# Fox attention normalised after the value product: blocks of ones beside the values give the row sums

## The chip, the core and the metric

The kernel runs on one core of a Trainium2 chip: TensorE (PE) for matrix products and transposes, VectorE (DVE) and ScalarE (ACT) for elementwise work, GpSimd (POOL), and queues that issue transfers (SP's and ACT's matter here). The engines run side by side and meet at semaphores. The metric is the device time of one execution in microseconds (us), of which the median of several runs is taken.

## The reference, cut to what matters

The kernel computes one step of a one-layer decoder: a projection into four branches, their merge, cross attention and a feed-forward part, for a prompt of 512 tokens and 8 sample tokens. The change touches branch D, the forgetting attention of the prompt: 8 heads of 64 over 512 tokens, causal.

```
def forgetting_attention(q, k, v, c_q, c_k, q_pos, k_pos):
    ...
        s = jnp.einsum('bqhd,bkhd->bhqk', qi, k, preferred_element_type=F32) * (d ** -0.5)
        s = s + jnp.swapaxes(ci, 1, 2)[..., None] - ck
        s = jnp.where(k_pos[None, None, None, :] <= pi[None, None, :, None], s, NEG_INF)
        p = jax.nn.softmax(s, axis=-1)
        return jnp.einsum('bhqk,bkhd->bqhd', p.astype(v.dtype), v)
```

## The kernel before

The weights of all projections are cut into pieces of 128 columns. For every piece `p` TensorE makes two halves (`("piece", p, 0)` and `("piece", p, 1)`), each of 24 products of 128x260 (12 for a piece of `w_branch` or `w_co`, whose weights have 512 rows): three products a block of rows, since weights and activations are split in a high and a low part (`wh`, `rawl`, `xh`, `xl`).

Everything else is a list of side steps, `SIDE`. The function `timeline()` puts one side step behind each half piece, and every engine walks the same list. The side step K works so: ACT and DVE do their part of step K on what TensorE left in PSUM in step K-1, and TensorE's part of step K waits for both (`act_s`, `dve_s`). While ACT and DVE work, TensorE does the half piece that stands between step K-1 and step K. So their part costs nothing as long as it is shorter than the half piece.

The steps of the stage are, in this order: `kvt` 0 to 4 transposes values and keys of the prompt, one block of 128 tokens a step, ACT copies the values into `vt` and the keys into `stg` and issues a store of each from its queue. `fc` makes the running sums of the forget gate. `fox` 0 to 34 is the attention, a pipeline over 32 (head, block of 128 queries) pairs. The logits of pair n are made in step n (PSUM bank `s0`, width w of 128, 256, 384 or 512 keys by the block, so the widths repeat with a period of four steps), the row maximum, the exponential into `fP` and the scaling in step n+1, the transpose of `fP` into bank `s1` also in step n+1, its copy to `fPT` and the product with `vt` into bank `s2` in step n+2, and the copy of `s2` to the branch's result `oD` in step n+3. Between them the paged values of the sample tokens pass (`("v", n)`, and `("vx", b)` each four of them). Their pages come by SP's queue, and DVE works on them at L1970 and L1974.

A step of DVE in `fox` is: row maximum (L1707), copy of the last but one pair's result (L1711), then wait for ACT's exponential, reciprocal of its 128x1 row sums (L1714), and the scaling of `fP` (the helper's line L1519). ACT has the exponential with the row sums as an accumulated second output (L1145) and then the copy to `fPT` (L1323).

The pieces end before the attention does. The steps `fox` 28 to 34 and then `df` (DVE, sample tokens) stand in the list without a half piece between them, because the pieces of branch D's own weights must come after. Then `split brD` follows: ACT copies `oD` to `oh`, DVE subtracts to get `ol`.

Of the kernel before, what the change touches and what calls it, by code (L numbers as in the profile page):

```python
# [18 lines left out]
ACT = mybir.ActivationFunctionType  # L19
# [382 lines left out]
def to_dve(s):  # L402

    kind, n = s[0], s[1]
    if kind == "fox":
        return int(1 <= n <= FOX)
    if kind == "x":
        return int(1 <= n <= XU)
    if kind == "l2" or kind == "gp":
        return int(n > 0)  # L410
    return {("sm", 2): 1, ("sm", 3): 1, ("fc", 1): 1, ("gdn", 0): 2, ("cln", 5): 1, ("cln", 6): 4, ("ds", 2): 1, ("dn", 1): 1,
            ("xd", 2): 1}.get((kind, n), 0)
# [19 lines left out]
def build(nc, a, out):  # L432
    ctx = ExitStack()
    with ctx:
# [144 lines left out]
        zrow = v(G + 1024, T)  # L579
        vt = v(G, QT, 512)  # L580
        fP, fPT = v(G + 2048, 512), v(G + 2560, QT, P)
        stg = v(G + 4096, 2, 512)
# [217 lines left out]
        def _(pe):  # L800
            def mm(o, l, r, start=True, stop=True):
                return pe.matmul(o, l, r, start=start, stop=stop, skip_group_check=True)  # L802
# [109 lines left out]
            def side(K, s):  # L912
# [56 lines left out]
                elif kind == "fox":  # L969
# [11 lines left out]
                    if 2 <= n <= FOX + 1:  # L981
                        h, q = divmod(n - 2, QT)
                        for b in range(q + 1):
                            last = mm(s2[FD * (h % 2):FD * (h % 2) + FD, 0:P], vt[:, b, h * FD:(h + 1) * FD], fPT[:, b, :], b == 0, b == q)
                elif kind == "l2":
# [152 lines left out]
        def _(act):  # L1138
# [5 lines left out]
            def fn(o, i, f, st=act_c, **kw):  # L1144
                own(act.activation(o, i, f, **kw), st)  # L1145
# [107 lines left out]
            def side(K, s):  # L1253
# [40 lines left out]
                elif kind == "kvt":  # L1294
                    j = (n - 1) % 2
                    rows = lambda x: x[0, (n - 1) * P:n * P].rearrange("t l h d -> t (l h d)")
                    fn(vt[:, n - 1, :], s0, ACT.Copy)
                    store(rows(out["fv_p"]), vt[:, n - 1, :], vt_out)
                    if used[j]:
# [16 lines left out]
                elif kind == "fox":  # L1316
                    if n <= FOX:
                        w = ((n - 1) % QT + 1) * P
                        act.wait_ge(v2a.sem, va + 1)
                        fn(fP[:, 0:w], s0[:, 0:w], ACT.Exp, a2v, bias=nmx[:, 0:1], accum_out=rsum[:, 0:1])  # L1320
                    w = ((n - 2) % QT + 1) if 2 <= n <= FOX + 1 else 1
                    if 2 <= n <= FOX + 1:
                        fins = act.activation(fPT[:, 0:w, :], s1[:, 0:w * P].rearrange("p (a b) -> p a b", a=w), ACT.Copy)  # L1323
                    else:
                        fins = act.activation(rsum[:, 1:2], eps6[:, 0:1], ACT.Copy)
                elif kind == "l2":
                    if n == 0:
# [75 lines left out]
                elif kind == "ml" and n == 0:  # L1403
                    act.wait_ge(gs_out, 16)
                    act.wait_ge(ss_st, 32)
                    act.wait_ge(vt_out, 64)
                    for j in range(2):
# [97 lines left out]
            act.wait_ge(ss_st, 32)  # L1505
            act.wait_ge(vt_out, 64)


        @block.vector
        def _(dve):  # L1510
# [146 lines left out]
            def side(K, s):  # L1657
# [46 lines left out]
                elif kind == "fox":  # L1704
# [3 lines left out]
                    if n >= 3:  # L1708
                        h, q = divmod(n - 3, QT)
                        r = slice(FD * (h % 2), FD * (h % 2) + FD)  # L1710
                        (dve_c if n <= FOX else dve_s).by(dve.tensor_copy(oD[r, h // 2, q * P:(q + 1) * P], s2[r, 0:P]))  # L1711
                    if n <= FOX:
                        dve.wait_ge(a2v.sem, av + 1)
                        own(dve.reciprocal(nmx[:, 1:2], rsum[:, 0:1]))  # L1714
                        ts(fP[:, 0:w], fP[:, 0:w], nmx[:, 1:2], st=dve_s)
                elif kind == "l2":
# [293 lines left out]
```

## Time and profile before

| | |
|---|---|
| median of 3 runs | 1835.05 us (1833.76 to 1837.18) |
| the profiled execution: its time, its span | 1833.14 us, 1831.3 us |
| busy over the span: PE, DVE, ACT, POOL | 84%, 51%, 30%, 27% |
| mean granted TensorE clock | 0.893 of full |
| the steps `kvt`, `fc` and `fox` lie at | about 836 to 1086 us of the span |

The busy share of PE is that of pipelined products, so it counts overlapping ones once and does not say that the engine is at its peak. The granted clock takes two values, full and half, and its mean says how much of the span was at each.

### The profile page before, as it was taken

Reading aid. Unit: us, or ns where it says so; the run is one execution under the profiler, and the core shown is the slowest. Engines: PE = TensorE matmul, PEld = TensorE weight load, DVE = VectorE, ACT = ScalarE, POOL = GpSimd, SP = SyncE. Lnnn points to the kernel's source line nnn. Section 1 sums busy time; section 2 is a strip of 40 time slices with the busy share of each in tenths; the row PEclk is TensorE's granted clock in tenths of the full one; section 3 lists DMA queues with packets and bytes.
Section 4 is the critical chain, followed back from the end, with each engine's and each line's share of the span. In section 5 each row is a group of like instructions: output and inputs, shape, how many; then the busy total and the mean of one; then the engine's idle time right before and its main releaser. Section 6 shows DMA issues by size and latency. Waiting matters only on the chain. (4 is left out here: it accounts for less than half of the span.)

```text
span 1831.3 us, 28404 instructions
## 1 busy us (share of the span) xinstructions
PE 1546.3 (84%) x11127; PEld 1424.3 (78%) x11127; DVE 942.1 (51%) x1421; ACT 555.5 (30%) x893; POOL 489.8 (27%) x286
## 2 busy tenths in 40 slices
PE   4896577878797978988899879889577999999996
PEld 4896577678796977877666659888476999999995
DVE  4169877999977754223222222264525566663122
ACT  3322441122224212263222232443214333333222
POOL 1253312234343400001111104310402444443440
PEclk8897786899898989999888879989757999999998
DMA  7145423433453416557343006432312233332331
GB/s 213 47 118 154 127 76 103 125 107 115 116 150 104 133 54 203 147 159 223 115 126 99 24 21 194 127 89 87 127 35 75 81 93 93 93 93 77 98 97 47
DMA packets 250997, 199.86 MB, mean 109 GB/s; under 512 B 11620, under 2 KB 208797, under 8 KB 250456
## 3 DMA queue, kind: packets, MB, share of 16 engines
q1 hardware_dynamic: 234149, 169.47, 31.9%
q10 hardware_dynamic: 15723, 23.86, 3.8%
q0 software_dynamic: 992, 4.72, 0.8%
q8 instruction: 88, 1.44, 0.3%
q14 instruction: 45, 0.37, 0.1%
HBM read 187.89 MB, written 10.81 MB: 108 GB/s over the span
## 5 line engine op out<-in xcount | busy, mean ns | idle before, releaser
L802 PE MATMUL pb<-xh,wh 128*128 128x260 f32 x2176 | 647.8, 298 | 48.7 <-DVE xl L1516 22.6
L802 PE MATMUL pb<-xl,wh 128*128 128x260 f32 x2176 | 631.9, 290 | 0.0
L802 PE MATMUL pb<-xh,rawl 128*128 128x260 f32 x2176 | 630.6, 290 | 0.0
L762 POOL TENSOR_TENSOR rawl<-raw,wh 128x1024 fp32r<-128x1024 f32 (+2 forms) x128 | 277.8, 2171 | 930.5 <-ACT wh L1145 930.3
L802 PEld LDWEIGHTS pb<-xh,wh 128*128 128x128 f32 x2176 | 428.5, 197 | 66.0 <-issue 34.9
L802 PEld LDWEIGHTS pb<-xl,wh 128*128 128x128 f32 x2176 | 428.4, 197 | 0.7
L802 PEld LDWEIGHTS pb<-xh,rawl 128*128 128x128 f32 x2176 | 427.7, 197 | 0.0
L1145 ACT ACTIVATE wh<-raw 128x1024 fp32r<-128x1024 f32 (+2 forms) x208 | 201.6, 969 | 557.0 <-PE pb L802 531.0
L802 PE MATMUL sd<-ar 128*128 128x128 f32 (+5 forms) x1584 | 282.7, 374 | 93.0 <-DVE ar L1516 33.8
L802 PEld LDWEIGHTS sd<-ar 128*128 128x128 f32 (+4 forms) x1584 | 199.9, 199 | 139.6 <-issue 78.1
L773 POOL TENSOR_TENSOR ar<-ar 128x512 f32<-128x512 f32 x128 | 182.2, 1423 | 333.1 <-DMA ar<-in_cache_fox_k 317.3
L1631 DVE TENSOR_TENSOR rawl<-raw,wh 128x1024 fp32r<-128x1024 f32 (+1 forms) x80 | 94.7, 1184 | 70.8 <-ACT wh L1145 70.6
L802 PE MATMUL pb<-oh,wh 128*128 128x260 f32 (+1 forms) x384 | 123.2, 321 | 7.3 <-ACT ar L1145 4.7
L802 PE MATMUL pb<-ol,wh 128*128 128x260 f32 (+1 forms) x384 | 116.7, 304 | 0.0
L802 PE MATMUL pb<-oh,rawl 128*128 128x260 f32 (+1 forms) x384 | 116.4, 303 | 0.0
L806 PE MATMUL sd<-cst,ar 128*128 128x128 f32 (+7 forms) x359 | 68.0, 316 | 51.6 <-DVE ar L1516 24.9
L802 PE MATMUL pb<-hh,wh 128*128 128x260 f32 x352 | 100.9, 287 | 2.6 <-DVE hl L1516 2.6
L1648 DVE SCALAR_TENSOR_TENSOR ar<-xT,cols,ar 128x512 f32<-128x512 f32 x120 | 102.0, 882 | 1.4 <-DVE ar L1516 0.3
L802 PE MATMUL pb<-hh,rawl 128*128 128x260 f32 x352 | 100.2, 285 | 0.0
L802 PE MATMUL pb<-hl,wh 128*128 128x260 f32 x352 | 100.1, 284 | 0.0
L1145 ACT ACTIVATE ar<-ar 128x520 f32<-128x520 f32 (+8 forms) x71 | 41.7, 587 | 190.2 <-DVE ar L1542 166.1
L1655 DVE TENSOR_REDUCE ar<-ar 128x8 f32<-128x512 f32 x128 | 85.2, 678 | 26.5 <-POOL ar L773 25.8
(168 smaller groups left out, 1756.9 us busy)
## 6 DMA issues: line engine op xcount, KB each, us to landing
raw<-in_w_in SPq DMA_DIRECT2D x80, 512.0 KB, 4.1
ar<-in_cache_fox_k SPq DMA_DIRECT2D x128, 256.0 KB, 2.7
ar<-in_cache_fox_v SPq DMA_DIRECT2D x128, 256.0 KB, 3.1
raw<-in_w_ffn_in SPq DMA_DIRECT2D x44, 512.0 KB, 3.7
raw<-in_w_branch SPq DMA_DIRECT2D x32, 256.0 KB, 3.2
raw<-in_w_ffn_out SPq DMA_DIRECT2D x16, 512.0 KB, 3.9
ar<-in_cache_mem_k ACTq DMA_DIRECT2D x1, 4096.0 KB, 19.2
raw<-in_w_out SPq DMA_DIRECT2D x8, 512.0 KB, 4.0
```

The source lines that it names most:

```text
L762: pool.tensor_tensor(rawl[:, p % RING, 0:kt, :], raw[:, p % RING, 0:kt, :], wh[:, p % (AHEAD + 1), 0:kt, :].bitcast(F32), SUB).then_inc(lo ...
L773: own(pool.tensor_tensor(kring[:, i % 4, :], kring[:, i % 4, :], qb[:, :], MUL), prod_done)
L802: return pe.matmul(o, l, r, start=start, stop=stop, skip_group_check=True)
L806: return pe.transpose(o, i, ident[0:n, 0:n])
L1145: own(act.activation(o, i, f, **kw), st)
L1631: dve.tensor_tensor(rawl[:, p % RING, 0:kt, :], raw[:, p % RING, 0:kt, :], wh[:, p % (AHEAD + 1), 0:kt, :].bitcast(F32), SUB).then_inc(lo. ...
L1648: dve_c.by(dve.scalar_tensor_tensor(out=oC[:, c, 0:SEQ], in0=g[:, j - 1:j - 1 + SEQ], scalar=w[:, j - 1:j], in1=oC[:, c, 0:SEQ], op0=MUL, ...
L1655: page_free.by(dve.tensor_reduce(sc[:, i, :], kring[:, i % 4, :].rearrange("p (h d) -> p h d", h=FH), AX, ADD))
```

## The change

The row sums no longer come from ACT's accumulator, and the exponentials are no longer scaled. The tile `vt` gets blocks of ones between the values of an even and an odd head (192 columns for two heads: 64 of values, 64 ones, 64 of values). The product for a head takes 128 of these columns where it took 64, so that its result has 64 partitions of sums of values and 64 of row sums. DVE takes the reciprocal of the 64x128 row sums, read from PSUM, into a new tile `frs`, and multiplies with it as it moves the result to `oD`. ACT does its copy to `fPT` first and the exponential after it. The values leave for DRAM in two stores of 256-byte rows for each block of tokens, instead of one of 2 KB rows.

```diff
--- before.py
+++ after.py
@@ -402,8 +402,6 @@
 def to_dve(s):
 
     kind, n = s[0], s[1]
-    if kind == "fox":
-        return int(1 <= n <= FOX)
     if kind == "x":
         return int(1 <= n <= XU)
     if kind == "l2" or kind == "gp":
@@ -577,8 +575,8 @@
         wsh = nc.alloc_sbuf_tensor_at("wsh", [P, KD, 16], F32R, offset=base + 4 * (G + 128))
         wsl = nc.alloc_sbuf_tensor_at("wsl", [P, KD, 16], F32R, offset=base + 4 * (G + 256))
         zrow = v(G + 1024, T)
-        vt = v(G, QT, 512)
-        fP, fPT = v(G + 2048, 512), v(G + 2560, QT, P)
+        vt = v(G, QT, 4 * 192)
+        fP, fPT, frs = v(G + 3072, 512), v(G + 3584, QT, P), v(SQ, P)
         stg = v(G + 4096, 2, 512)
 
         cnh = nc.alloc_sbuf_tensor_at("cnh", [P, 512], F32R, offset=base + 4 * (G + 5632))
@@ -981,7 +979,7 @@
                     if 2 <= n <= FOX + 1:
                         h, q = divmod(n - 2, QT)
                         for b in range(q + 1):
-                            last = mm(s2[FD * (h % 2):FD * (h % 2) + FD, 0:P], vt[:, b, h * FD:(h + 1) * FD], fPT[:, b, :], b == 0, b == q)
+                            last = mm(s2[:, 0:P], vt[:, b, 192 * (h // 2) + FD * (h % 2):192 * (h // 2) + FD * (h % 2) + 2 * FD], fPT[:, b, :], b == 0, b == q)
                 elif kind == "l2":
                     for j in range(2):
                         for h in range(2):
@@ -1294,8 +1292,11 @@
                 elif kind == "kvt":
                     j = (n - 1) % 2
                     rows = lambda x: x[0, (n - 1) * P:n * P].rearrange("t l h d -> t (l h d)")
-                    fn(vt[:, n - 1, :], s0, ACT.Copy)
-                    store(rows(out["fv_p"]), vt[:, n - 1, :], vt_out)
+                    vb = vt[:, n - 1, :].rearrange("p (c e d) -> p c e d", c=4, e=3)
+                    fn(vb[:, :, 1, :], spread(ones[:, 0:FD], 4, 1), ACT.Copy)
+                    for e in range(2):
+                        fn(vb[:, :, 2 * e, :], s0.rearrange("p (c e d) -> p c e d", c=4, e=2)[:, :, e, :], ACT.Copy)
+                        store(rows(out["fv_p"]).rearrange("t (c e d) -> t c e d", c=4, e=2)[:, :, e, :], vb[:, :, 2 * e, :], vt_out)
                     if used[j]:
                         act.wait_ge(stg_out[j], 16 * used[j])
                     fn(stg[:, j, :], s1, ACT.Copy)
@@ -1314,15 +1315,19 @@
                     fn(pn[:, :, :], pn[:, :, :], ACT.Exp, a2v)
                     fins = act.activation(rsum[:, 0:1], eps6[:, 0:1], ACT.Copy)
                 elif kind == "fox":
-                    if n <= FOX:
-                        w = ((n - 1) % QT + 1) * P
-                        act.wait_ge(v2a.sem, va + 1)
-                        fn(fP[:, 0:w], s0[:, 0:w], ACT.Exp, a2v, bias=nmx[:, 0:1], accum_out=rsum[:, 0:1])
+                    if n == 1:
+                        act.wait_ge(ss_st, 32)
                     w = ((n - 2) % QT + 1) if 2 <= n <= FOX + 1 else 1
                     if 2 <= n <= FOX + 1:
                         fins = act.activation(fPT[:, 0:w, :], s1[:, 0:w * P].rearrange("p (a b) -> p a b", a=w), ACT.Copy)
                     else:
                         fins = act.activation(rsum[:, 1:2], eps6[:, 0:1], ACT.Copy)
+                    if n <= FOX:
+                        act_c.by(fins)
+                        w = ((n - 1) % QT + 1) * P
+                        act.wait_ge(v2a.sem, va + 1)
+                        act.wait_ge(act_c.sem, act_c.n)
+                        fins = act.activation(fP[:, 0:w], s0[:, 0:w], ACT.Exp, bias=nmx[:, 0:1])
                 elif kind == "l2":
                     if n == 0:
                         act.wait_ge(qs_out, 16)
@@ -1403,7 +1408,7 @@
                 elif kind == "ml" and n == 0:
                     act.wait_ge(gs_out, 16)
                     act.wait_ge(ss_st, 32)
-                    act.wait_ge(vt_out, 64)
+                    act.wait_ge(vt_out, 128)
                     for j in range(2):
                         act.wait_ge(stg_out[j], 16 * used[j])
                     act.dma_start(mrow[:, :, :], a["mem_prompt"][0].rearrange("(t p) d -> p t d", p=P)).then_inc(mem_in, 16)
@@ -1503,7 +1508,7 @@
             act.wait_ge(ss_out, 16)
             act.wait_ge(gs_out, 16)
             act.wait_ge(ss_st, 32)
-            act.wait_ge(vt_out, 64)
+            act.wait_ge(vt_out, 128)
 
 
         @block.vector
@@ -1708,11 +1713,11 @@
                     if n >= 3:
                         h, q = divmod(n - 3, QT)
                         r = slice(FD * (h % 2), FD * (h % 2) + FD)
-                        (dve_c if n <= FOX else dve_s).by(dve.tensor_copy(oD[r, h // 2, q * P:(q + 1) * P], s2[r, 0:P]))
-                    if n <= FOX:
-                        dve.wait_ge(a2v.sem, av + 1)
-                        own(dve.reciprocal(nmx[:, 1:2], rsum[:, 0:1]))
-                        ts(fP[:, 0:w], fP[:, 0:w], nmx[:, 1:2], st=dve_s)
+                        rs_ = slice(FD - FD * (h % 2), 2 * FD - FD * (h % 2))
+                        own(dve.reciprocal(frs[r, :], s2[rs_, 0:P]))
+                        tt(oD[r, h // 2, q * P:(q + 1) * P], s2[r, 0:P], frs[r, :], MUL, dve_s)
+                    else:
+                        fin()
                 elif kind == "l2":
                     dve.wait_ge(a2v.sem, av + 1)
                     for j in range(2):
```

DVE in the last `fox` steps, before and after. The `TENSOR_REDUCE` is the row maximum of step n, `sd` is PSUM, `ar` is the large SBUF tile that holds `fP`, `frs` and `oD`.

```order
L1707 TENSOR_REDUCE ar<-sd 128x1
L1711 COPY ar<-sd 64x128
L1714 RECIPROCAL ar<-ar 128x1
L1519 TENSOR_SCALAR ar<-ar 128x384
L1707 TENSOR_REDUCE ar<-sd 128x1
L1711 COPY ar<-sd 64x128
L1714 RECIPROCAL ar<-ar 128x1
L1519 TENSOR_SCALAR ar<-ar 128x512
L1711 COPY ar<-sd 64x128 x2
L1516 TENSOR_TENSOR ar<-ar 64x4x8
```

```order
L1712 TENSOR_REDUCE ar<-sd 128x1
L1717 RECIPROCAL ar<-sd 64x128
L1521 TENSOR_TENSOR ar<-sd,ar 64x128
L1712 TENSOR_REDUCE ar<-sd 128x1
L1717 RECIPROCAL ar<-sd 64x128
L1521 TENSOR_TENSOR ar<-sd,ar 64x128
L1717 RECIPROCAL ar<-sd 64x128
L1521 TENSOR_TENSOR ar<-sd,ar 64x128
L1717 RECIPROCAL ar<-sd 64x128
L1521 TENSOR_TENSOR ar<-sd,ar 64x128
L1521 TENSOR_TENSOR ar<-ar 64x4x8
```

Each step has three instructions of DVE where it had four, none of them behind ACT's exponential, and the reciprocal has 128 elements a partition where it had one. The last two steps and `df` (which begins with the `64x4x8` row) have the reciprocal and the product where there was a copy.

ACT in a `kvt` step, before and after: one block of tokens.

```order
L1145 ACTIVATE ar<-sd 128x512
L1245 DMA out_fv_p<-ar 128x512
L1145 ACTIVATE ar<-sd 128x512
L1245 DMA out_fk_p<-ar 128x512
L1303 ACTIVATE ar<-ar 128x1
```

```order
L1143 ACTIVATE ar<-cst 128x4x64
L1143 ACTIVATE ar<-sd 128x4x64
L1243 DMA out_fv_p<-ar 512x1x64
L1143 ACTIVATE ar<-sd 128x4x64
L1243 DMA out_fv_p<-ar 512x1x64
L1143 ACTIVATE ar<-sd 128x512
L1243 DMA out_fk_p<-ar 128x512
L1304 ACTIVATE ar<-ar 128x1
```

Three activations of 256 elements stand where one of 512 did, with one more store issued between them, all ahead of the step's last instruction, which TensorE waits for.

## Rows read from the trace of the kernel before

**Rows 1.** Windows: us, busy of each engine, clock, DMA share, GB/s

```profile
1058.00:1086.00 28.00, 19.07 (x57) 11.48 (x58) 5.99 (x20) 5.45 (x15) 0.00 (x0) 0.52 0.03 8
...
856.00:860.00 4.00, 4.00 (x35) 2.96 (x35) 0.17 (x1) 1.83 (x3) 0.00 (x0) 1.00 1.08 364
```

**Rows 2.** Waits of PE, 820 to 1100 us: total, times, longest

```profile
PE sd L802 <- DVE ar L1519: 22.6, 11, 2.9
...
PE sd L802 <- ACT ar L1323: 2.4, 2, 1.6
```

**Rows 3.** Timeline, a step 512 wide (start, us, engine, line) [idle before]

```profile
1077.54 0.69 DVE L1707 TENSOR_REDUCE ar<-sd 128x1 f32<-128x512 f32 x1 [5.54 <-PE sd L802]
1078.26 0.29 DVE L1711 COPY ar<-sd 64x128 f32<-64x128 f32 x1
...
1079.35 0.49 DVE L1519 TENSOR_SCALAR ar<-ar 128x512 f32<-128x512 f32 x1
...
1078.34 0.69 ACT L1145 ACTIVATE ar<-sd,ar 128x512 f32<-128x512 f32 x1 [6.58 <-DVE ar L1707]
...
1079.98 1.09 PE L806 MATMUL sd<-cst,ar 128*128 128x128 f32 x4 [2.54 <-DVE ar L1519]
```

**Rows 4.** Timeline, the three steps before it, 128, 256 and 384 wide

```profile
1057.94 0.29 DVE L1707 TENSOR_REDUCE ar<-sd 128x1 f32<-128x128 f32 x1 [3.05 <-PE sd L802]
...
1058.35 0.37 ACT L1145 ACTIVATE ar<-sd,ar 128x128 f32<-128x128 f32 x1 [3.65 <-DVE ar L1707]
...
1059.49 1.22 PE L802 MATMUL sd<-ar 64*128 64x256 f32 x2 [1.64 <-ACT ar L1323]
...
1064.05 0.42 DVE L1707 TENSOR_REDUCE ar<-sd 128x1 f32<-128x256 f32 x1 [4.73 <-PE sd L802]
...
1065.89 1.62 PE L802 MATMUL sd<-ar 64*128 64x384 f32 x2 [1.93 <-DVE ar L1519]
...
1070.00 0.56 DVE L1707 TENSOR_REDUCE ar<-sd 128x1 f32<-128x384 f32 x1 [4.26 <-PE sd L802]
...
1072.14 2.04 PE L802 MATMUL sd<-ar 64*128 64x512 f32 x2 [2.23 <-DVE ar L1519]
```

**Rows 5.** Groups of DVE by form: xcount | busy us, mean ns

```profile
L1711 DVE COPY ar<-sd 64x128 f32<-64x128 f32 x32 | 9.1, 283 | 5.6 <-PE sd L802 5.2
L1714 DVE RECIPROCAL ar<-ar 128x1 f32<-128x1 f32 x32 | 5.3, 164 | 17.0 <-ACT ar L1145 17.0
...
L1867 DVE RECIPROCAL ar<-ar 128x64 f32<-128x64 f32 x1 | 0.6, 554 | 0.0
...
L1912 DVE RECIPROCAL ar<-sd 128x32 f32<-128x32 f32 x1 | 0.4, 358 | 28.1 <-PE sd L802 28.1
```

**Rows 6.** Timeline of the attention's end

```profile
1082.64 0.29 DVE L1711 COPY ar<-sd 64x128 f32<-64x128 f32 x1 [2.80 <-PE sd L802]
...
1083.28 1.97 PE L802 MATMUL sd<-ar 128*64 128x128 f32 x8 [0.74 <-ACT ar L1323]
...
1085.64 2.47 DVE L1516 TENSOR_TENSOR ar<-ar 64x32 f32<-64x32 f32 x6
...
1088.41 2.65 ACT L1145 ACTIVATE oh<-ar 128x520 fp32r<-128x520 f32 x4 [1.58 <-DVE cols L1525]
```

**Rows 7.** Timeline of PE: value products, and products of branch B

```profile
902.06 1.09 PE L802 MATMUL sd<-ar 128*64 128x128 f32 x8
...
513.21 1.05 PE L802 MATMUL sd<-ar 128*128 128x128 f32 x8
```

**Rows 8.** Timeline of a kvt step on ACT and the next on PE

```profile
843.45 0.60 ACT L1145 ACTIVATE ar<-sd 128x512 f32<-128x512 f32 x1 [0.21 <-PE sd L806]
844.08 0.34 ACTq L1245 DMA_DIRECT2D out_fv_p<-ar  x1
...
845.48 0.20 ACT L1303 ACTIVATE ar<-ar 128x1 f32<-128x1 f32 x1 [0.42 <-ACT ar L1145]
...
847.15 1.09 PE L806 MATMUL sd<-cst,ar 128*128 128x128 f32 x8
```

## The prediction

> **What bounds the kernel now.** I began with the windows of the stage. In its last 28 us TensorE had half a clock and was busy for 19.07 of them, so something else sets the pace there [rows 1]. The waits of TensorE name it. Eleven times it waited for DVE's scaling of the exponentials, 22.6 us in all, and twice for ACT's copy, 2.4 us [rows 2]. A further 2.54 us fell on its transposes for the same scaling [rows 3]. That is 14 waits and 27.5 us in 35 steps. In the other steps the chain hides behind a half piece. I matched the starts of the row maxima to the list of steps: of the 14 waits, two are at a step 128 wide, five at one 256 wide, three at 384, three at 512, and the last is at the second-last result, which has no row maximum. Elsewhere TensorE is the engine that the rest waits for, so what such a wait loses comes back one to one in the time.
>
> The chain at an exposed step is row maximum, exponential, row sum, reciprocal, scaling, TensorE. At a width of 512 it took from 1077.54 to 1079.98, 2.44 us [rows 3]. At 384 it took 2.14, at 256 it took 1.84, at 128 it took 1.55 [rows 4]. The reader is to see that four instructions of two engines stand one behind the other, and DVE's copy of a result is inside, hidden beside the exponential.
>
> **What the change puts there.** ACT's path becomes row maximum, exponential, TensorE. The exponential started 0.80 us after the row maximum at 512 [rows 3] and 0.41 at 128 [rows 4], and takes 0.69 and 0.37. With 0.14 us from the end of the last instruction to TensorE (0.49 after 1079.35, then 1079.98) that path has 1.63 us at 512 and 0.92 at 128. ACT's copy now stands in front, beside DVE's row maximum. At 128 wide it is the 0.60 us copy of 512 elements, so that the exponential would end at 0.64 + 0.37, and the path has 1.15.
>
> DVE's path becomes row maximum, reciprocal of 64x128, product of 64x128, TensorE, and this one is longer. The profile has no reciprocal of this size. It has three smaller ones: 164 ns with one element a partition, 554 ns with 64, 358 ns with 32 read from PSUM [rows 5]. The slope is (554 - 164) / 63 = 6.2 ns an element, and the PSUM one gives (358 - 164) / 31 = 6.3, so that 128 elements cost 164 + 127 x 6.2 = 0.95 us. The number of partitions does not enter. The lower bound is the copy of the same 64x128 from PSUM, 0.28 us [rows 5]. I take 0.95, because two rows of the same operation agree on the slope, one of them from the same memory. The product is priced as that copy, 0.29. With 0.04 between the two for the wait of the second on the first, what follows the row maximum is 0.95 + 0.04 + 0.29 + 0.14 = 1.42 us.
>
> The Trainium skill, "VectorE: DVE Perf Modes", section "Walkthrough: the 8-slice pipeline in each mode", says that the reciprocal is an iterated hardware divide with a repeat count of 8. An estimate from that count at VectorE's 0.96 GHz is 8.3 ns an element, 1.22 us for the instruction, which would add 0.27 us at each exposed step and some 3 us in all. The rows give 6.2 ns, and the sum goes by them.
>
> The reciprocal can start where the copy started: 0.72 after the row maximum's start at 512 [rows 3], and about 0.59, 0.34 and 0.21 at the other widths, the row maximum (0.56, 0.42, 0.29 [rows 4]) and a few hundredths or less. Exposed steps then take:
>
> 512 wide: 0.72 + 1.42 = 2.14 against 2.44, -0.30, three times: -0.90. 384 wide: 2.01 against 2.14, -0.13, three times: -0.39. 256 wide: 1.76 against 1.84, -0.08, five times: -0.40. 128 wide: 1.63 against 1.55, +0.08, once. The other one 128 wide is the first step, before there is a result to normalise; it goes by ACT's path with ACT's short stand-in for the copy, 0.92 against 1.55: -0.63. One more step of 128 had almost no cover left and may now show 0.15.
>
> **The end of the attention gets longer.** In the second-last step TensorE waited 0.74 us for ACT's copy, which began with DVE's at 1082.64 and was over before 1083.28 [rows 6]. Now it waits for 1.42, so +1.42 - 0.64 = +0.78. In the last step the 0.29 copy becomes 0.95 + 0.04 + 0.29, which is +0.99 on DVE ahead of the six products of `df` (2.47 us), after which ACT splits the result [rows 6]. TensorE has one piece's half as cover there, 24 products, which ended with `df` and not after it, so I count all 0.99.
>
> The sum over the attention is -0.90 - 0.39 - 0.40 + 0.08 - 0.63 + 0.15 + 0.78 + 0.99 = -0.32 us.
>
> **What else is added.** The value products take 128 columns of weights where they took 64. Eight records of the 64-column form took 1.09 us, eight of the full form in branch B 1.05 [rows 7]; I count nothing. It is bounded by the weight load, which overlaps.
>
> Each of the four `kvt` steps on ACT gets three activations of 256 elements for one of 512. One of 128 elements takes 0.37 [rows 4], one of 512 takes 0.60 [rows 8], so one of 256 about 0.45. With one more store issued (0.34) and three gaps of 0.04 a step grows by 1.35 + 0.34 + 0.12 - 0.60 = 1.21 us. The step shown ended at 845.68, and TensorE came for it at 847.15 [rows 8], so 1.47 us of cover is left and 0.26 of it remains. ACT also has evacuations and splits of weights behind these steps, and all of its slack there goes. If a step has 0.1 to 0.2 less cover than this one TensorE stands for that time; I count +0.3 for all four, between 0 and 4 x 1.21 if there were no cover.
>
> The two stores have rows of 256 bytes, 4096 of them in place of 512 of 2 KB, while the DMA engines are saturated (share 1.08 at 364 GB/s around 858 us [rows 1]). The pages of the sample's values come at the same time, and `fc` waits for them through DVE. The bytes do not grow; if a row of 256 bytes were as slow as one of 512, the 1.05 MB would count as 2.1, and 1.05 MB at 364 GB/s are 2.9 us at most. I count +0.3, since it matters only for the pages that are waited for. The Trainium skill, "DMA: Bandwidth & Descriptors", section "Specifications", speaks against these stores: below 512 bytes a transfer is a read-modify-write and not at line rate. No run here shows that yet.
>
> Sum: -0.32 + 0.3 + 0.3 = +0.3 us on the profiled execution's 1833.14, so 1833.4. The median of the runs stands 1.9 above that execution, which gives 1835.3.
>
> **The rivals.**
>
> *Faster: the reciprocal costs little.* If it streams like the copy (0.28), DVE's path is 0.67 us shorter and ACT's path decides: 1.63 at 512, and about 1.4, 1.2 and 1.15 at the others. The waits lose 3 x 0.8, 3 x 0.7, 5 x 0.6, 0.4 and 0.6, the end gains nothing and loses nothing, together -8.5 us, and stretches of half clock get rarer, which could give 2 more: 1825. For it speaks only that the instruction is of the usual kind; against it the three rows with one slope. Chance 0.07.
>
> *Faster: the clock.* Half clock is granted after the waits, and the last 28 us had a mean of 0.52 [rows 1]. Where the waits shrink by 0.3 us, a stretch of half clock may not come, and products that ran at half speed are given back; eight records of the value product take 1.09 us at full clock [rows 7]. Most exposed steps keep waits of 1.7 to 2.6 us, so I expect the stretches to stay. It decides from three stretches on, at 1 to 2 us each: 1831. Chance 0.10.
>
> *Slower: ACT overflows in `kvt`.* If strided copies or the issue of 256-byte stores cost 0.2 us more than I take, the step grows by some 1.8 us, over the 1.47 of cover. TensorE stands 0.3 to 0.6 us in four steps, pages come later with it, `fc` follows, and one or two stretches of half clock are added: 2 + 3 = 5 us, 1840. It decides when a step on ACT grows by more than 1.47 us. For it speaks the full DMA share, against it that the issue took 0.34 for a full store. Chance 0.15.
>
> *No change that can be measured*, my forecast: 0.68.
>
> **How the numbers follow.** A measurement of this kernel can tell about 0.2% from no change, 3.7 us. Under 1831.4 is faster, over 1838.7 slower. My forecast's own range is 1832.5 to 1838.5, by the bounds of the `kvt` and store terms (0 to +3) and of the clock (2 either way). The range to both rivals of 0.10 and 0.15, leaving out less than 2 in 10, is 1830.5 to 1839.5. From the cases: faster 0.07 + 0.10 = 0.17, slower 0.15, the same 0.68.
>
> **What would show it.** In the changed profile the reciprocal of 64x128 at 0.95 us; DVE's product, not ACT's exponential, as the releaser of TensorE in the exposed steps, with waits near 2.2 at 512 wide; no accumulator reads in the attention; a wait near 1.5 where 0.74 stood; ACT's split of the result 1.5 to 2 us later against the attention's begin. I am wrong if TensorE's waits for the attention fall under 20 us in all, if TensorE stands in `kvt` for over 1 us in all, or if the waits for pages before `fc` grow by over 1 us.

## The result, and the profile of the changed kernel

The changed kernel is faster: a median of 1825.23 us (4 runs, 1823.88 to 1826.67) against 1834.64 for the kernel before beside it (4 runs, 1833.76 to 1837.18). The ratio is 0.9946, with a 95% interval of 0.992 to 0.9972: 9.4 us less. I had forecast 1835.3 and gave "faster" 0.17, and my range began at 1830.5, so the prediction was wrong, in its number and in its sign. The profiled execution took 1825.85 us with a span of 1824.1; the mean granted clock is 0.893, as before.

**The chain of DVE is what I forecast.** The groups of DVE by form (xcount | busy us, mean ns), which answer to [rows 5], have the reciprocal at 955 ns, where I had 0.95 us, and the product at 289:

```profile
L1717 DVE RECIPROCAL ar<-sd 64x128 f32<-64x128 f32 x32 | 30.6, 955 | 5.8 <-PE sd L800 4.9
L1521 DVE TENSOR_TENSOR ar<-sd,ar 64x128 f32<-64x128 f32 x32 | 9.2, 289 | 1.1
```

The timeline of the last step 512 wide, which answers to [rows 3]:

```profile
1068.82 0.69 DVE L1712 TENSOR_REDUCE ar<-sd 128x1 f32<-128x512 f32 x1 [5.34 <-PE sd L800]
1069.54 0.95 DVE L1717 RECIPROCAL ar<-sd 64x128 f32<-64x128 f32 x1
1069.54 0.69 ACT L1330 ACTIVATE ar<-sd,ar 128x512 f32<-128x512 f32 x1 [0.24 <-DVE ar L1712]
1070.52 0.29 DVE L1521 TENSOR_TENSOR ar<-sd,ar 64x128 f32<-64x128 f32 x1
1070.96 1.09 PE L804 MATMUL sd<-cst,ar 128*128 128x128 f32 x4 [2.24 <-DVE ar L1521]
```

From 1068.82 to 1070.96 are 2.14 us, the forecast to the hundredth at this width. The waits of TensorE from 820 to 1100 us, which answer to [rows 2] (us in total, times, longest):

```profile
PE sd L800 <- DVE ar L1521: 24.1, 13, 2.8
PE sd L804 <- DVE ar L1521: 4.9, 2, 2.7
...
PE sd L800 <- ACT ar L1330: 1.1, 1, 1.1
```

One of the two waits of L804 (2.7) lies in an earlier step and stands in the profile of before too. The attention's own are 24.1 + 2.2 + 1.1 = 27.4 us, where there were 27.5. So the waits gave nothing in sum (some fell and some rose, see below), and the whole gain lies where TensorE works.

**How long the attention is.** I measure it on TensorE from the first logits to the first transposes behind it; these transposes wait for nothing in either kernel: 869.26 to 1088.72 before, 219.5 us, and 868.50 to 1081.04 now, 212.5. The stage begins 0.8 us earlier and what follows is 0.5 longer: -0.8 - 6.9 + 0.5 = -7.2 us, the whole difference of the two spans.

**Where it was found.** The timeline of TensorE and its weight loads in one step with a value product over four blocks, at full clock. Kernel before:

```profile
954.99 0.29 PE L806 MATMUL sd<-cst,ar 128*128 128x128 f32 x1
955.21 0.85 PEld L802 LDWEIGHTS sd<-ar 128*64 128x64 f32 x8
955.21 1.09 PE L802 MATMUL sd<-ar 128*64 128x128 f32 x8
956.23 0.18 PEld L802 LDWEIGHTS pb<-xh,wh 128*128 128x128 f32 x1 [0.17 <-issue]
956.23 0.39 PE L802 MATMUL pb<-xh,wh 128*128 128x260 f32 x1
```

Changed kernel, the same step:

```profile
953.18 0.29 PE L804 MATMUL sd<-cst,ar 128*128 128x128 f32 x1
953.18 0.99 PEld L800 LDWEIGHTS sd<-ar 128*128 128x128 f32 x8
953.31 1.06 PE L800 MATMUL sd<-ar 128*128 128x128 f32 x8
954.10 0.19 PEld L800 LDWEIGHTS pb<-xh,wh 128*128 128x128 f32 x1
954.12 0.37 PE L800 MATMUL pb<-xh,wh 128*128 128x260 f32 x1
```

The reader is to look at the starts, not at the durations. From the start of the transposes to that of the first product of the next half piece are 1.24 us before and 0.94 now. The run itself is nearly the same, 1.09 us before and 1.06 now, which is all that [rows 7] could show; but before it the gap is 0.22 against 0.13, and from its start to the next product 1.02 against 0.81. In the kernel before the first load of the run starts with its first product, 0.22 us after the transposes, and the load behind the run stands for 0.17 of issue and starts with its product too. Now both loads start ahead of their products, beside the work before them (953.18 for 953.31, 954.10 for 954.12). That is 0.30 us a step, in 32 steps 9.6 us. In the other steps at full clock with a half piece behind them the same difference is 0.29 to 0.32, whether one, two, three or four blocks are multiplied.

The Trainium skill, "TensorEngine Tiling (Array Packing)", section "Key Properties", says that a change of the tiling mode drains TensorE. That section gives no price, and doesn't say that an operand of 64 columns is such a mode by itself. The two timelines agree with the rule if it is, at 0.30 us for a run between full-width ones; that a drain is what stands in the two gaps is not shown.

**The steps `kvt` and the end.** Rows of the changed kernel for a `kvt` step on ACT, with the last wait of TensorE in them, answering to [rows 8]:

```profile
843.66 0.42 ACT L1143 ACTIVATE ar<-cst 128x256 f32<-128x256 f32 x1 [0.33 <-PE sd L804]
...
844.52 0.54 ACTq L1243 DMA_DIRECT2D out_fv_p<-ar  x1
...
847.16 0.20 ACT L1304 ACTIVATE ar<-ar 128x1 f32<-128x1 f32 x1 [0.45 <-ACT ar L1143]
...
860.71 0.60 PE L804 MATMUL sd<-cst,ar 128*8 128x128 f32 x4 [0.38 <-ACT ar L1304]
```

ACT's part takes 3.70 us where it took 2.23 (843.45 to 845.68), +1.47 against the +1.21 that I had, since the issue of such a store takes 0.54 and not 0.34 (+0.40 for the two), while the three activations took 0.16 less than I had put them at. It used up the cover, and TensorE stood 0.38 us once.

The end of the attention, answering to [rows 6]:

```profile
1073.42 0.95 DVE L1717 RECIPROCAL ar<-sd 64x128 f32<-64x128 f32 x1 [2.60 <-PE sd L800]
...
1074.85 2.05 PE L800 MATMUL sd<-ar 128*128 128x128 f32 x8 [1.52 <-DVE ar L1521]
...
1080.76 2.65 ACT L1143 ACTIVATE oh<-ar 128x520 fp32r<-128x520 f32 x4 [2.28 <-DVE cols L1530]
```

The wait is 1.52 where it was 0.74, as forecast, and from DVE's part in that step to ACT's split are 7.34 us against 5.77, +1.57 where I had +1.77.

### The profile page after: what moved, and what is told of

Its sections match the earlier page's. It is cut to its first block and busy times, and to the rows that moved or that the text cites. A ratio compares the mean times of both kernels' runs of the same rounds, so it can differ in the third digit from the quotient of the medians.

```text
span 1824.1 us, 28355 instructions
## 1 busy us (share of the span) xinstructions
PE 1535.7 (84%) x11127; PEld 1427.0 (78%) x11127; DVE 958.6 (53%) x1391; ACT 555.4 (30%) x869; POOL 490.8 (27%) x286
## 5 line engine op out<-in xcount | busy, mean ns | idle before, releaser
L800 PE MATMUL sd<-ar 128*128 128x128 f32 (+4 forms) x1584 | 280.7, 375 | 95.9 <-DVE ar L1521 55.9
L800 PEld LDWEIGHTS sd<-ar 128*128 128x128 f32 (+3 forms) x1584 | 205.7, 207 | 134.8 <-issue 74.0
L804 PE MATMUL sd<-cst,ar 128*128 128x128 f32 (+7 forms) x359 | 65.9, 308 | 53.1 <-DVE ar L1521 27.6
```

The source lines that it names most:

```text
L804: return pe.transpose(o, i, ident[0:n, 0:n])
```

## The experiments

The theory: the 64-column operand costs TensorE 0.30 us in each step, and its removal is the gain. The rivals: the shorter chain and its clock; the `kvt` edit; a chance shift of the stretches of half clock.

**The wide product alone.** The kernel before with a value product over the 128 columns of the pair of heads; the half that isn't wanted lands on the other 64 partitions and is not read.

```diff
-  last = mm(s2[FD * (h % 2):FD * (h % 2) + FD, 0:P], vt[:, b, h * FD:(h + 1) * FD], fPT[:, b, :], b == 0, b == q)
+  last = mm(s2[:, 0:P], vt[:, b, 128 * (h // 2):128 * (h // 2) + 128], fPT[:, b, :], b == 0, b == q)
```

> The kernel before with one edit: the value product takes the 128 value columns of the head's pair (64 of this head, 64 of its neighbour) as weights, so that its result fills all 128 partitions; VectorE copies only this head's 64 as before. Softmax sums, scaling, stores and layout are those of before. Theory A (TensorE pays for going into and out of its 64-column form): in the traces, transposes to value products to next product take 0.26 + 1.02 us before and 0.13 + 0.81 after for four blocks, about 0.3 us a step at full clock and 0.45 at half clock, 32 steps: minus 10 us, 1824 to 1825. Rival B (the gain comes from taking the scaling of the exponentials off the chain): 1834 to 1835, no change. Rival C (the granted clock): any value, but with a mean clock clearly over 0.893.

Median 1828.03 against 1835.79, ratio 0.9974 (0.9949 to 0.9999), profiled 1825.0. The attention is 209.0 us long (869.73 to 1078.72), 10.5 less than before, with the old chain and nearly its old waits (23.0 + 2.5 + 2.6 = 28.1 us, 0.6 more: two waits begin earlier by what TensorE gained and end with the same chain, and a third shows for the first time). Summed over the 30 steps that have transposes and a value product, the stretch from the transposes to the next product is 10.0 us shorter, nearly all of the 10.5. One line gives the whole shortening of the stage. The interval of the median is wide and its upper end is close to no change: one of the twelve runs took 1847.12 us, and the quotient of the two medians is 0.9958. The attention's length is the firmer reading, though it is that of one execution.

**The change with the narrow product.** The changed kernel with 64 columns; the row sums are left out and the reciprocal is taken of the 64x128 weighted values themselves, so that every other instruction stands with its size. The result is no attention; only the time is of use.

```diff
-  last = mm(s2[:, 0:P], vt[:, b, 192 * (h // 2) + FD * (h % 2):192 * (h // 2) + FD * (h % 2) + 2 * FD], ...)
+  last = mm(s2[FD * (h % 2):FD * (h % 2) + FD, 0:P], vt[:, b, 192 * (h // 2) + 2 * FD * (h % 2):... + FD], ...)
-  own(dve.reciprocal(frs[r, :], s2[rs_, 0:P]))
+  own(dve.reciprocal(frs[r, :], s2[r, 0:P]))
```

> The changed kernel with one edit: the value product takes only the head's own 64 columns of values, so the row sums are left out, and the reciprocal is taken of the same 64 partitions of the result. Instructions on VectorE, ScalarE and the queues are those of the changed kernel, in number, size and order. Theory A: the 10 us come back, 1834 to 1836, with a value product that is again followed by a gap of some 0.2 us. Rival B (chain): stays at 1825.

Median 1838.61, ratio 1.0026 (1.0013 to 1.004): slower than the kernel before by 2 to 7 us. The attention is 224.5 us (865.72 to 1090.24), 12.0 more than in the changed kernel. The gain is gone with the width, so neither the chain nor `kvt` brought it; together they cost something. The waits don't show that cost (23.1 + 2.2 + 1.1 = 26.4 us); the mean clock is lower, 0.79 in the attention against 0.82.

**More narrow runs, and their control.** In the kernel before, transposes and value products in turn, block by block, so that there are more narrow runs between full-width records and no more work. The control has the same order with 128 columns.

```diff
-  if 1 <= n <= FOX:
-      for b in range((n - 1) % QT + 1):
-          last = tr(...)
-  if 2 <= n <= FOX + 1:
-      for b in range(q + 1):
-          last = mm(...)
+  for b in range(QT):
+      if b < trs:
+          last = tr(...)
+      if 2 <= n <= FOX + 1 and b <= q:
+          last = mm(...)
```

> The kernel before with TensorE's value products and transposes of one step taken in turn (one transpose, one value product, ...), in place of all transposes and then all value products; nothing else moves. Value products come in runs of 1, 2, 3 and 4; in turn with 2, 3, 4 and 1 transposes they make 1, 2, 3 and 2 runs of the 64-column form in four steps where there were 4, so 32 more in all. Theory A: plus 32 x 0.3 to 0.45, 1844 to 1849. Rivals B and C: no change, 1834 to 1836.

> The kernel before with both edits: 128 columns of weights in the value product, and value products and transposes in turn. The control of the run before it: if the order itself cost something it would show here. Theory A: as the wide kernel alone, 1824 to 1825. If the order costs by itself: the same rise as in the narrow one.

The narrow one: 1845.26, ratio 1.0051 (1.0033 to 1.0068), attention 232.0 us. The control: 1826.54, ratio 0.9957 (0.9943 to 0.9971), attention 210.7. The order alone does nothing (210.7 beside 209.0 of the wide product in the old order); with 64 columns it costs 21.3. The timelines of TensorE price one run. Narrow:

```profile
948.30 0.43 PE L802 MATMUL sd<-ar 128*64 128x128 f32 x2
948.66 0.33 PE L806 MATMUL sd<-cst,ar 128*128 128x128 f32 x1
948.92 0.43 PE L802 MATMUL sd<-ar 128*64 128x128 f32 x2
```

Wide:

```profile
949.61 0.39 PE L802 MATMUL sd<-ar 128*128 128x128 f32 x2
949.83 0.27 PE L806 MATMUL sd<-cst,ar 128*128 128x128 f32 x1
949.94 0.39 PE L802 MATMUL sd<-ar 128*128 128x128 f32 x2
```

Two products and a transpose take 0.62 us a turn with 64 columns and 0.33 with 128: 0.29 us for each narrow run, the 0.30 of the first timelines. The old order has four such runs in four steps and this one seven, so 56 for 32 in all: 24 more, and not the 32 more of my expectation, which gave the steps with one transpose and four products two runs where they have one. The time fell into the expected range by luck, since the 24 cost 12.5 us of attention, more than 0.45 each. Against the control, 56 x 0.29 are 16.2 of the 21.3 us; the rest goes with a lower clock (a mean of 0.80 against 0.82), at which a run costs more.

**The `kvt` part alone.** The kernel before with `vt` in the layout with ones, three activations and two stores of values a step, and a narrow product.

```diff
-  fn(vt[:, n - 1, :], s0, ACT.Copy)
-  store(rows(out["fv_p"]), vt[:, n - 1, :], vt_out)
+  fn(vb[:, :, 1, :], spread(ones[:, 0:FD], 4, 1), ACT.Copy)
+  for e in range(2):
+      fn(vb[:, :, 2 * e, :], s0.rearrange("p (c e d) -> p c e d", c=4, e=2)[:, :, e, :], ACT.Copy)
+      store(rows(out["fv_p"])...[:, :, e, :], vb[:, :, 2 * e, :], vt_out)
```

> The kernel before with only the new layout of the values: blocks of ones between the heads, three small copies and two stores of 256-byte rows per block of tokens; the value product stays at 64 columns, the softmax as before, and the ones are not used. It prices the part of the change in the kvt steps. By the prediction's term: 0.3 to 0.6 us, 1835 to 1836. In the changed kernel's trace the issue of such a store takes 0.54 to 0.65 us where 0.34 stood, and a kvt step on ScalarE 3.7 us where 2.2 stood, yet TensorE waited 0.4 us once, so I expect at most plus 1. Rival: the four steps and the later page loads cost 2 to 5 us, which would explain why the changed kernel's attention is 3.6 us longer than that of the wide kernel.

Median 1838.33 against 1838.01, ratio 0.9997 (0.9982 to 1.0011), attention 220.1 us. My +0.3 for ACT and +0.3 for the stores are not told from nothing. At most 2 us of the 2 to 7 of the narrow-product run can be of this part; the rest is left to the new chain by elimination, and no run has the chain alone.

**The chain's signal given early.** The changed kernel, with the results of the last steps in two PSUM banks in turn, so that DVE can let TensorE go before it normalises.

```diff
-  last = mm(s2[:, 0:P], ...)
+  last = mm((s3 if n >= 25 and n % 2 else s2)[:, 0:P], ...)
...
+  sx = s3 if n - 1 >= 25 and (n - 1) % 2 else s2
+  early = 25 <= n <= FOX + 1
+  if early:
+      dve_s.by(dve.tensor_copy(fl8[:, 0:1], fl8[:, 1:2]))
   own(dve.reciprocal(frs[r, :], sx[rs_, 0:P]))
-  tt(oD[r, h // 2, q * P:(q + 1) * P], s2[r, 0:P], frs[r, :], MUL, dve_s)
+  tt(oD[r, h // 2, q * P:(q + 1) * P], sx[r, 0:P], frs[r, :], MUL, dve_c if early else dve_s)
```

> The changed kernel; in the last steps (25 to 34) the value product goes to the banks s2 and s3 in turn, and VectorE tells TensorE that it may go on before it takes the reciprocal and the product, in place of after them. Theory: in the changed kernel the 64x128 reciprocal (0.955 us) and the product (0.29) stand in front of TensorE; without them ScalarE's path is left, so the six waits there fall by 0.4 to 0.8 us each, minus 3 us in all, about 1822 (on this chip, with the changed kernel at 1825). Rival (ScalarE's path is as long): no change.

Median 1817.53, ratio 0.989 (0.9871 to 0.9909); the attention is 205.8 us (867.04 to 1072.80), 6.8 less than in the changed kernel. I had expected 3. Of the 6.8, TensorE's waits are 4.7 (22.7 us for 27.4); the other 2.1 have no cause that I can show. Its timeline of the last step 512 wide:

```profile
1062.21 0.69 DVE L1712 TENSOR_REDUCE ar<-sd 128x1 f32<-128x512 f32 x1 [4.52 <-PE sd L800]
1062.93 0.15 DVE L1720 COPY cols<-cols 128x1 f32<-128x1 f32 x1
1062.94 0.69 ACT L1330 ACTIVATE ar<-sd,ar 128x512 f32<-128x512 f32 x1 [0.24 <-DVE ar L1712]
1063.12 0.95 DVE L1721 RECIPROCAL ar<-sd 64x128 f32<-64x128 f32 x1
1063.68 1.11 PE L804 MATMUL sd<-cst,ar 128*128 128x128 f32 x4 [1.56 <-ACT ar L1330]
```

The reciprocal still takes 0.95 but lies beside TensorE's work; the step shows 1.47 us (1062.21 to 1063.68) instead of 2.14. The whole kernel is some 20 us below the kernel before, where the changed kernel is 9 to 10 below. The normalisation behind the product pays once nothing waits for it.

**The other narrow operands.** Two more kinds are in each step: the queries and keys on 64 rows, and the bias rows (`cnh`, `cnl`) on 8. On top of the wide product alone, the bias products get 128 rows with added rows of zeros, which ACT writes in the last `kvt` step (not shown; `sel` gives 128 rows too):

```diff
-  mm(s0[:, 0:w], sel(h), cnh[0:FH, 0:w], False, False)
-  mm(s0[:, 0:w], sel(h), cnl[0:FH, 0:w], False, False)
+  mm(s0[:, 0:w], sel(h), cnh[:, 0:w], False, False)
+  mm(s0[:, 0:w], sel(h), cnl[:, 0:w], False, False)
```

> The wide kernel, and the two products that add the forget gate's sums to the logits take all 128 rows (the 120 further ones are zeros) where they took 8. Theory A in its wide form (every change of the array's form costs, rows too): in the wide kernel's trace the logits' two records take 0.41 us where two such records take 0.22 elsewhere, and the step from the 8-row products to the mask 0.26 where 0.12 is usual. A step then has two changes of form where it had three, minus 0.13 to 0.19 us in 32 steps: minus 4 to 6 us against the wide kernel, 1818 to 1821. Narrow form of A (only the number of columns counts): 1824, as the wide kernel.

and then the logits too, with a copy of the queries whose other 64 rows are zero, made by DVE in `kvt` 2 and `fc` 0 (not shown):

```diff
-  mm(s0[:, 0:w], fq[r, h // 2, q * P:(q + 1) * P], fk[r, h // 2, 0:w], True, False)
+  mm(s0[:, 0:w], qkv[:, 8 * (h % 2) + h // 2, q * P:(q + 1) * P], fk[:, h // 2, 0:w], True, False)
```

> The kernel before it, and the logits take 128 rows too: VectorE makes, ahead of the attention and in idle time, a copy of the queries for even and one for odd heads in which the other head's rows are zero. No product of the attention changes the array's form any more. Theory A in its wide form: three changes a step saved against the wide kernel, 0.2 + 0.19 + 0.13 = 0.5 us at full clock in 32 steps and more at half clock, minus 16 to 20 us against the wide kernel, 1805 to 1809. Narrow form: 1824. Rival: the copies of 4.4 us each on VectorE delay the page sums and the attention starts later, plus 2 to 4.

The first: 1819.7, ratio 0.9896 (0.9878 to 0.9915), attention 205.4 us. The second: 1795.59, ratio 0.9774 (0.9757 to 0.9792), attention 179.8 us (873.05 to 1052.89). It is 24 us below the first, more than I had expected of it (1805 to 1809). The timelines of TensorE in a step 512 wide at full clock show a part. With bias rows alone:

```profile
1041.50 1.12 PE L802 MATMUL sd<-ar 64*128 64x512 f32 x2
...
1043.18 0.49 PE L806 MATMUL sd<-cst,ar 128*128 128x128 f32 x3
```

With all rows:

```profile
1022.88 1.02 PE L802 MATMUL sd<-ar 128*128 128x512 f32 x2
...
1024.26 0.49 PE L806 MATMUL sd<-cst,ar 128*128 128x128 f32 x3
```

From the logits to the transposes are 1.68 and 1.38 us (1.87 with the wide product alone), so 0.30 a step from the logits on, and the same at the other three widths. The start of the logits itself comes 0.21 us after that of the half piece's last product with bias rows alone and 0.13 with all rows, which is another 0.08. So 0.38 a step, 12 of the 25.6 us in 32 steps. The rest goes with the clock: the mean over the attention is 0.93, and was 0.81 with the bias rows alone. The windows of the last stretch (us, busy of each engine, clock, DMA share, GB/s), first bias rows, then all rows; the second holds more steps:

```profile
1052.00:1077.00 25.00, 17.56 (x68) 13.70 (x67) 7.24 (x21) 5.81 (x14) 1.27 (x1) 0.52 0.00 0
```

```profile
1023.00:1053.00 30.00, 20.91 (x131) 18.55 (x130) 11.16 (x32) 9.00 (x22) 1.28 (x1) 0.89 0.07 18
```

Over the same steps, from the last logits 128 wide to the end, the mean clock is 0.61 in the first (1046.90 to 1077.43) and 0.86 in the second (1027.90 to 1052.89). TensorE waits as often and as long as ever (24.1 + 2.5 + 2.6 us in the attention); only the clock differs. In each run eleven waits of 1.6 us and more stand ahead of logits; the products behind them ran at half clock ten times with bias rows alone and three times with all rows. One of these pairs, the same step with the same wait, first bias rows, then all rows:

```profile
1060.71 2.04 PE L802 MATMUL sd<-ar 64*128 64x512 f32 x2 [2.23 <-DVE ar L1523]
```

```profile
1039.26 1.10 PE L802 MATMUL sd<-ar 128*128 128x512 f32 x2 [2.23 <-DVE ar L1523]
```

It is no chance of one execution: the mean clock of the whole span is 0.899 to 0.906 in all thirteen executions with all rows (here and below) and at most 0.898 in every other. Nor are shorter steps by themselves the cause, since the wide product took 0.30 us off a step and the bias rows 0.14 to 0.20, and the attention's mean clock stayed at 0.81 to 0.83. The price of the zeros and copies is not measured: the attention starts at 872.03 and 873.05 in these two, and at 867.04 and 867.17 in the two runs above on the same chip, but the start moves between 865.72 and 871.25 among the kernels without them. In the two combined runs below TensorE waits 4.6 us for the running sums ahead of the first logits, where it was 3.1.

**Repeats and combinations.** Four kernels on one chip: the changed kernel again; it with one activation for both heads' values and the ones written in `fc` 0 (the last two lines of the diff), so that ACT's `kvt` step is shorter; it with all operands on 128 rows; and that with the early signal.

```diff
-  fn(vb[:, :, 1, :], spread(ones[:, 0:FD], 4, 1), ACT.Copy)
+  fn(vb[:, :, 0:3:2, :], s0.rearrange("p (c e d) -> p c e d", c=4, e=2), ACT.Copy)
   for e in range(2):
-      fn(vb[:, :, 2 * e, :], s0...[:, :, e, :], ACT.Copy)
       store(...)
...
+  for t in range(QT):
+      fn(vt[:, t, :]...[:, :, 1, :], spread(ones[:, 0:FD], 4, 1), ACT.Copy)
```

> The changed kernel itself, unedited, beside the other three on one chip. Theory (the gain is the wide value product's 0.30 us a step at full clock, 0.46 at half): 8 to 11 us below the kernel before, ratio 0.994 to 0.9955. It gives the base for the next three.

> The changed kernel with the ones written in the step fc 0 and the values of both heads moved by one strided copy, so that ACT's kvt step is 0.8 to 0.9 us shorter; the two stores of 256-byte rows stay. In the changed kernel the first attention step ran at half clock and its attention took 3.6 us longer than that of the kernel before with only the wide product. If the longer kvt step brings that, this kernel has the full clock at the first attention step and is 2 to 4 us faster than the changed kernel. If the new order of the attention's chain brings it, or if it is chance, it is within 1 us of it.

> The changed kernel with every operand of the attention's products on 128 rows, the added rows zero. The same edit took the kernel before with a wide value product from an attention of 209.0 us to 179.8 and by 32 us in the median. Theory (products on 64 and 8 rows cost time in themselves and bring the half clock): attention of 178 to 184 us, median 30 to 34 us below the changed kernel, about 1793. Rival (the two edits of the normalisation and the rows share their gain, since with the full clock DVE's longer path is what shows): under 26 us below it, 1799 or more.

> The kernel with the early signal in the last nine attention steps, with all operands on 128 rows too. The early signal took 6.8 us off the attention of the changed kernel. If that was DVE's reciprocal and product leaving the path of TensorE, it is worth the same here: 5 to 8 us below the run with the rows alone, 1786 to 1790. If it was the clock, it is worth 0 to 3 us here, since the clock is mostly full then.

The changed kernel: 1825.7, ratio 0.9945 (0.9929 to 0.9962), the result again and as expected. The shorter `kvt` step: 1827.42, ratio 0.9962 (0.9946 to 0.9977), attention 211.9 us beside 211.8; its first attention step is still at half clock (0.76 us for the two products that take 0.46 at full). So the length of the `kvt` step isn't what puts half clock there. The narrow run with transposes and products in turn has the old `kvt` steps and half clock in that step too (0.77), so no part of the change is needed for it. With all rows: 1798.48, ratio 0.9792 (0.9754 to 0.9831), but the four runs lie between 1793.6 and 1806.2, and the profiled one is the slowest of them (attention 188.9 us, mean clock 0.87); its median lies below the rival's 1799 and above the theory's 1793, and tells neither (27.2 below the changed kernel, where the theory had 30 to 34 and the rival under 26). With the early signal too: 1795.6, ratio 0.9789 (0.9754 to 0.9825), profiled 1788.6 with an attention of 177.8 us and a clock of 0.92. Its interval covers the one without the signal, so the 5 to 8 us that I expected are not shown here, though TensorE's waits in the attention are 4.5 us fewer again (24.5 for 28.9). The best ratio of all is that of the kernel before with the wide product and all rows, 0.9774, and the two last ones are not told from it: with all rows, what the change adds to a wide product is not shown to be worth anything.

## Why the prediction was wrong

**The step that failed** is this one: "The value products take 128 columns of weights where they took 64. Eight records of the 64-column form took 1.09 us, eight of the full form in branch B 1.05 [rows 7]; I count nothing." The two durations are right and the conclusion isn't, since the price lies in the gaps at both ends of the run and not inside it: 0.09 us ahead of it and 0.21 behind. The next sentence, that the weight load overlaps, is what fails there: in the kernel before the loads at those two places didn't. The term was 0 and measured -10.5 us in the attention (the wide product alone) and -12.0 (the changed kernel against its narrow form). None of my rivals had it. Why a load of 64 columns isn't begun beside the work before it stays open.

**The chain** was right in mechanism: 955 ns, 2.14 us at 512 wide, DVE's product as the releaser, the wait of 1.52. Its sum was right only by luck. The waits changed by -0.1 us in all, and I had -0.32, but that held +0.99 for the last step, which shows in no wait of TensorE; without it I had -1.31. The last half piece covered it, and took 0.9 us longer itself, since more of it ran at half clock (from its first product to the attention's end 4.49 us, 3.58 with the wide product alone). The terms for 512 and 384 wide and for the second-last result came out to 0.01 us.

The other terms were mis-sized. The five waits at 256 wide changed by +0.62 and not by -0.40: I had let the reciprocal start 0.34 us after the row maximum's start, where the copy did, but that row maximum takes 0.42, and the reciprocal started 0.46 after it (1055.80, 1056.26); and two of the five rose by 0.25, of which 0.21 came with the wide product alone, since TensorE is there earlier. At 128 wide the same error (0.21 for 0.32) turned my +0.08 into +0.20. The first step gave -0.78 for -0.63, and the newly exposed one 0.41 for 0.15.

Against my test that I am wrong if these waits fall under 20 us, they didn't: the test looked at the wrong place.

**The rival of a cheap reciprocal** is refuted by 955 ns. That its time, 1825, is the measured one is chance: its mechanism gave nothing of it. My estimate from the repeat count in the Trainium skill, "VectorE: DVE Perf Modes", section "Walkthrough: the 8-slice pipeline in each mode", was 1.22 us; the measurement decides for the slope of the rows, 0.95.

**The clock** went the other way than in my rival. The narrow-product run is 2 to 7 us slower than the kernel before with waits 1.1 us shorter; its attention has a mean clock of 0.79 against 0.82. In the changed kernel it shows in the first steps: from 866 to 880 us the clock was 0.58 where it had been 0.69. By windows of before and after:

```profile
866.00:880.00 14.00, 9.04 (x44) 7.81 (x43) 5.48 (x12) 3.99 (x10) 2.37 (x1) 0.69 0.34 102
```

```profile
866.00:880.00 14.00, 10.45 (x41) 9.18 (x42) 3.87 (x10) 3.82 (x8) 2.36 (x1) 0.58 0.35 111
```

The changed kernel's attention is 3.6 us longer than that of the wide product alone, with 27.4 and 28.1 us of waits. Counted from the first logits, 1.0 of it is lost by the second transposes (883.80 against 884.00), 1.7 by those at 1048.87 (1048.39), and the last 1.8 mostly with the wait at the second-last result (+0.78) and the last half piece (+0.9). Mean clocks of 0.81 and 0.83 over 212 and 209 us are some 81 and 71 us at half clock (twice the missing share, times the length). What shifts these stretches stays open: the `kvt` part alone also had half clock in its first step (and no slower attention for it), so had a run with the old `kvt` part, shortening that part didn't take it away, and the chain wasn't run apart from the layout of `vt`. Chance isn't ruled out, though the changed kernel's attention was about as long in its second profile (211.8 us).

**`kvt` and the stores**: a size was off (+1.47 a step for +1.21), and TensorE stood 0.38 us, under my limit of 1. The `kvt` part alone measured 0.9997. The step stood just at the condition of the overflow rival (+1.47), and its 5 us did not come. The rule of the Trainium skill against rows under 512 bytes ("DMA: Bandwidth & Descriptors", section "Specifications") had no consequence that this kernel could show, within the 0.1 to 0.2% of that run; the stores landed after a median of 4.1 us for 3.8, and the issue took longer, 0.54 for 0.34 us.

**ACT's split** was to come 1.5 to 2 us later against the attention's begin and came 6.9 earlier (212.3 us for 219.2). Counted from the second-last result the forecast holds, +1.57.

## What to carry to other kernels

To price a change in the shape of a matrix product, read the starts of the records in front of it and behind it, not its own duration: a run on 64 columns, 64 rows or 8 rows between full ones cost some 0.2 to 0.4 us here, most of it outside the records of the run. If the missing columns or rows lie beside the operand anyway, or can be zeros written once, take them: here a wide product and zero rows gave 2.3% where the elaborate change gave 0.5%. A normalisation behind a product is worth having when TensorE is let go before it.

## What the runs showed of the hardware

- A run of 64-column products between full-width ones costs 0.29 to 0.30 us at full clock (0.62 against 0.33 us a turn). At half clock, a step over three blocks took 2.47 us from the transposes to the next product before (979.45 to 981.92) and 2.01 in the changed kernel (976.32 to 978.33): 0.46.
- Products on 64 and 8 rows cost too, at full clock: 0.14 to 0.20 us a step for the bias rows, 0.38 for the logits (0.08 of it ahead of them).
- With all operands on 128 rows the mean granted clock of the attention rose from 0.81 to 0.93, with waits as long as before. I had taken half clock for a consequence of the waits alone. That the shape of the products takes part is shown by these runs; how, is not.
- DVE's reciprocal from PSUM costs 955 ns for 128 elements a partition, on the slope of [rows 5].
